# Dilated attention in pairs of heads: 64-row score products and eight units of work in place of sixteen

## What is computed

```python
n = rms_norm(h, ln_mix_g[l])
proj = n @ w_in[l]
qa, ka, va, qb, kb, vb, ga, gb = jnp.split(proj, splits, axis=-1)
qa = rope(qa.reshape(b, s, A_HEADS, HEAD_DIM), pos)      # 12 heads of 64
ka = rope(ka.reshape(b, s, A_HEADS, HEAD_DIM), pos)
ya = dilated_mixture(qa, ka, va).astype(h.dtype) @ w_branch_a[l]
```

## Time and profile before

| | |
|---|---|
| median of 3 runs | 3610.61 us |
| lowest, highest | 3605.58, 3610.79 us |
| span of the profiled execution | 3613.3 us |
| TensorE, VectorE, ScalarE busy | 3363.9, 1851.0, 1178.6 us |
| mean granted TensorE clock | 0.959 |

### The profile page before, as it was taken

The page is one execution under the profiler, slowest core; times in us unless marked ns, Lnnn a source line. Parts: engine busy times, 40 slices in busy tenths (PEclk is TensorE's granted clock), DMA queues, the critical chain, the costliest instruction groups (busy, mean ns, idle before and its releaser), DMA issues. The chain is left out here.

```text
span 3613.3 us, 51777 instructions
## 1 busy us (share of the span) xinstructions
PE 3363.9 (93%) x22874; PEld 2722.1 (75%) x22874; DVE 1851.0 (51%) x2262; ACT 1178.6 (33%) x1475; POOL 71.9 (2%) x50
## 2 busy tenths in 40 slices
PE   8999998999999999999999979999698778899996
PEld 7777777788778887987788857888376766588885
DVE  5344565677344435363644265443744765654436
ACT  3224544322232223432322243222323333232223
POOL 0000000000000001000100011000000000100001
PEclk9898999999999999999999999999698899899998
DMA  4111122222222223222222322322122000122231
GB/s 156 59 36 35 47 105 82 73 103 86 89 93 94 101 88 114 82 82 99 83 104 83 104 70 82 105 83 86 43 82 80 4 4 15 53 94 100 84 107 47
DMA packets 44463, 283.71 MB, mean 79 GB/s; under 512 B 5184, under 2 KB 5456, under 8 KB 18384
## 3 DMA queue, kind: packets, MB, share of 16 engines
q1 hardware_dynamic: 44240, 280.41, 22.5%
HBM read 278.29 MB, written 2.10 MB: 78 GB/s over the span
## 5 line engine op out<-in xcount | busy, mean ns | idle before, releaser
L460 PE MATMUL ps<-xh,wh 128*128 128x512 f32 x2464 | 982.4, 399 | 86.0 <-DVE xl L935 34.9
L460 PE MATMUL ps<-xl,wh 128*128 128x512 f32 x2464 | 971.3, 394 | 0.0
L460 PE MATMUL ps<-xh,wl 128*128 128x512 f32 x2464 | 970.7, 394 | 0.0
L313 DVE TENSOR_TENSOR wl<-raw,wh 128x2048 fp32r<-128x2048 f32 (+3 forms) x284 | 591.3, 2082 | 465.2 <-ACT wh L308 464.9
L460 PEld LDWEIGHTS ps<-xh,wh 128*128 128x128 f32 x2464 | 467.5, 190 | 217.1 <-issue 85.4
L308 ACT CAST wh<-raw 128x2048 fp32r<-128x2048 f32 (+3 forms) x284 | 492.1, 1733 | 307.3 <-PE ps L460 302.0
L460 PEld LDWEIGHTS ps<-xh,wl 128*128 128x128 f32 x2464 | 467.6, 190 | 102.1 <-issue 2.7
L460 PEld LDWEIGHTS ps<-xl,wh 128*128 128x128 f32 x2464 | 468.5, 190 | 97.5 <-issue 2.4
L460 PE MATMUL ps<-hid_h,wh 128*128 128x512 f32 x880 | 346.1, 393 | 2.7 <-DVE wl L313 2.7
L460 PE MATMUL ps<-hid_h,wl 128*128 128x512 f32 x880 | 346.4, 394 | 0.0
L460 PE MATMUL ps<-hid_l,wh 128*128 128x512 f32 x880 | 346.0, 393 | 0.0
(11 more groups left out here) (382 smaller groups left out, 4020.4 us busy)
## 6 DMA issues: line engine op xcount, KB each, us to landing
raw<-in_up SPq DMA_DIRECT2D x88, 1024.0 KB, 4.9
raw<-in_down SPq DMA_DIRECT2D x64, 704.0 KB, 4.0
raw<-in_up_c SPq DMA_DIRECT2D x22, 1024.0 KB, 4.8
raw<-in_down_c SPq DMA_DIRECT2D x16, 704.0 KB, 4.1
raw<-in_gates SPq DMA_DIRECT2D x8, 1024.0 KB, 4.9
raw<-in_gv SPq DMA_DIRECT2D x8, 1024.0 KB, 4.9
raw<-in_gu SPq DMA_DIRECT2D x8, 1024.0 KB, 4.9
raw<-in_gout SPq DMA_DIRECT2D x8, 1024.0 KB, 4.9
```

Of the source, the lines that this page charges most:

```text
L313: nc.vector.tensor_tensor(wl[:, slot, 0:w], raw[:, slot, 0:w], wh[:, slot, 0:w].bitcast(F32), ALU.subtract).then_inc(lo_ready, 1)
L460: last = nc.tensor.matmul(out, stationary, moving, start=(fresh and q == 0), stop=(t == kt - 1 and half == per - 1 and q == 2), skip_group ...
```

## The change

`rotate` writes its two results into a new buffer, `turned_rows`. ScalarE then issues eight DMAs per chunk of q or k, 48 in all, which copy 32 rows each into `qk` so that each head has its two halves below each other in 64 rows: heads 0 and 2 of a group in rows 0 to 63, heads 1 and 3 in rows 64 to 127 of two tiles. A score is then one product of 64 rows. The units become 8, of a pair of heads and a block b, in the order b = 0, 3, 1, 2, each with 12 fill steps. Every step of a unit handles both heads: scores and `weigh` alternate between them, in different banks and row halves (scores) or in different column halves (`weigh`). The masks of a group are added to both heads' scores in one instruction. The exponentials, the normalising and the turning stay one per head; normalising is now in place. The scores of a unit are issued in two parts and each waits for the group two before it; the lots of a turn hold 2 to 4 blocks. In units 0 and 4 the split of the next chunk comes ahead of the copies and behind the mask.

```diff
-    rope = area("rope", [P, 2, T], 44 * KB)
-    dil = area("dil", [P, GROUPS, T + 384], 48 * KB)
+    dil = area("dil", [P, GROUPS, T + 384], 44 * KB)
+    turned_rows = area("turned_rows", [P, 2 * GROUPS, 2, T], 54 * KB + 512)
+    rope = area("rope", [P, 2, T], 78 * KB + 512)
...
-            nc.vector.tensor_tensor(tile(qk, k * 2 + first_tile), tmp[:, 0, :], tmp[:, 1, :],
+            nc.vector.tensor_tensor(turned_rows[:, first_tile // 2 + k, 0, :], tmp[:, 0, :], tmp[:, 1, :],
                                     ALU.subtract).then_inc(dve_steps.sem, 1)
...
+    def place_heads(first_tile):
+        def part(act, k, products, u):
+            act.wait_ge(dve_steps.sem, dve_steps.after(k, 6))
+            for half in range(2):
+                for j in range(GH):
+                    row = HD * (j % 2) + HD // 2 * half
+                    act.dma_start(qk[row:row + HD // 2, first_tile + 2 * k + j // 2, :],
+                                  turned_rows[32 * j:32 * j + 32, first_tile // 2 + k, half, :]).then_inc(heads_placed, 16)
+        return part
+
+    linear("qa", KD, 256, x_split, act_part=place_heads(0), dve_part=rotate(0), steps=(0, 6), norms=first_norm)
...
-    units = [(j, b) for j in range(GH) for b in range(TB)]
+    units = [(pair, b) for pair in range(GH // 2) for b in (0, 3, 1, 2)]
+    LAST = len(units) - 1
...
+    LOT_SIZES = {0: ([3], [3]), 1: ([3, 3], [3, 3]), 2: ([3, 3, 2], [3, 3, 2]), 3: ([4, 3, 3], [3, 4, 3])}
...
+    def turn_bank(lot, size):
+        return ps[:, 6, 0:size * P] if lot % 2 == 0 else ps[:, 7, P:P + size * P]
+
+    def score_bank(u, g, e):
+        return 1 + 2 * ((GROUPS * u + g) % 2) + e
...
+        pe.wait_ge(heads_placed, HEADS_PLACED)
...
+    def opens(u):
+        return u * PER % (2 * KD) == 0
+
     @block.tensor
     def _(pe):
+        def scores(u, g):
+            pair, b = units[u]
+            step = GROUPS * u + g
+            if step >= 2:
+                pe.wait_ge(da_masked.sem, da_masked.base + step - 1)
+            k0, n = key_span(g, b)
+            for e in range(2):
+                rows = slice(HD * e, HD * e + HD)
+                last = nc.tensor.matmul(ps[:, score_bank(u, g, e), 0:n], qk[rows, 2 * g + pair, b * P:(b + 1) * P],
+                                        qk[rows, 2 * GROUPS + 2 * g + pair, k0:k0 + n], start=True, stop=True)
             last.then_inc(da_scores.sem, 1)
+        def turn(u, e):
+            pe.wait_ge(da_norm.sem, da_norm.after(u, e + 1))
+            for lot, first_block, size in turn_lots(u, e):
+                if lot >= 2:
+                    pe.wait_ge(da_moved.sem, da_moved.base + lot - 1)
...
         def weigh(u):
...
+            for n, (g, kb_) in enumerate(every):
+                for e in range(2):
+                    head = (g * GH + 2 * pair + e) * HD
+                    last = nc.tensor.matmul(ps[HD * e:HD * e + HD, 7, 0:P], va[:, kb_, head:head + HD],
+                                            probs_t[:, e, n * P:(n + 1) * P], start=(n == 0), stop=(n == len(every) - 1),
+                                            skip_group_check=True)
...
+        scores(0, 0)
+        scores(0, 1)
+        fill(0, 0, 2)
+        scores(0, 2)
         for u in range(len(units)):
+            if u < LAST:
+                scores(u + 1, 0)
+                scores(u + 1, 1)
+            fill(u, 0 if u else 2, 5)
             turn(u, 0)
+            if u < LAST:
+                scores(u + 1, 2)
+            fill(u, 5, 8)
             turn(u, 1)
+            fill(u, 8, PER)
             weigh(u)
...
+                nc.vector.tensor_tensor(masked[u % 2][:, :, off[g]:off[g + 1]], score_pair(u, g, n),
+                                        dil[:, g, m0:m0 + n].unsqueeze(1).broadcast_to([P, 2, n]),
+                                        ALU.add).then_inc(da_masked.sem, 1)
...
         for u in range(len(units)):
             normalise(u)
+            if u < LAST:
                 mask(u + 1)
+            if opens(u):
+                rows_of, unit = begun(u)[0]
+                rows_of.low(dve, unit // 2)
             for rows_of, unit in ended(u):
                 if rows_of is not vb_tokens:
                     rows_of.evict(dve, unit)
             low(u)
```

More of the change, by code:

```diff
@@ L1355, in begun @@
         return LOTS[(u * PER + KD - 1) // KD:((u + 1) * PER + KD - 1) // KD]
+    def opens(u):
+        return u * PER % (2 * KD) == 0
     @block.tensor
     def _(pe):
[L1359 to L1369, removed]
-            last.then_inc(da_scores.sem, 1)
@@ new lines, in turn @@
+        def turn(u, e):
[3 more added lines that the diff above has]
+                    pe.wait_ge(da_moved.sem, da_moved.base + lot - 1)
+                if u and lot == lots_before[u] + 1:
+                    pe.wait_ge(da_low.sem, da_low.after(u - 1, 1))
+                bank = turn_bank(lot, size)
+                for n in range(size):
+                    c0 = (first_block + n) * P
+                    last = nc.tensor.transpose(bank[:, n * P:(n + 1) * P], masked[u % 2][:, e, c0:c0 + P], table("ident"))
+                last.then_inc(da_turned.sem, 1)
@@ L1383, in weigh @@
         def weigh(u):
-            j, b = units[u]
-            pe.wait_ge(da_moved.sem, da_moved.after(u, 3))
+            pair, b = units[u]
+            pe.wait_ge(da_moved.sem, da_moved.base + lots_before[u + 1])
             if u:
                 pe.wait_ge(da_low.sem, da_low.after(u - 1, 1))
-            rows = slice(HD * (j % 2), HD * (j % 2) + HD)
-            every = [x for lot in key_blocks(b) for x in lot]
+            every = key_blocks(b)
             for n, (g, kb_) in enumerate(every):
-                head = (g * GH + j) * HD
-                last = nc.tensor.matmul(ps[rows, 7, 0:P], va[:, kb_, head:head + HD],
-                                        probs_t[:, n * P:(n + 1) * P], start=(n == 0), stop=(n == len(every) - 1))
+                for e in range(2):
[3 more added lines that the diff above has]
+                                            skip_group_check=True)
@@ L1435, in normalise @@
             n = offsets(units[u][1])[3]
-            dve.wait_ge(da_exp.sem, da_exp.after(u, 1))
-            nc.vector.reciprocal(stat[:, u % 2, 3:4], stat[:, u % 2, 2:3]).then_inc(da_rec.sem, 1)
+            dve.wait_ge(da_exp.sem, da_exp.after(u, 2))
+            nc.vector.reciprocal(stat[:, u % 2, 3, :], stat[:, u % 2, 2, :]).then_inc(da_rec.sem, 1)
             dve.wait_ge(da_rec.sem, da_rec.after(u, 1))
[L1439 to L1442, removed]
+            for e in range(2):
+                nc.vector.tensor_scalar(masked[u % 2][:, e, 0:n], masked[u % 2][:, e, 0:n], stat[:, u % 2, 3, e:e + 1], None,
+                                        ALU.mult).then_inc(da_norm.sem, 1)
         def low(u):
-            j, b = units[u]
-            rows, cols = slice(HD * (j % 2), HD * (j % 2) + HD), slice(b * P, (b + 1) * P)
+            pair, b = units[u]
+            cols = slice(b * P, (b + 1) * P)
             dve.wait_ge(da_high.sem, da_high.after(u, 1))
-            nc.vector.tensor_tensor(ya_l[rows, j // 2, cols], ps[rows, 7, 0:P], ya_h[rows, j // 2, cols].bitcast(F32),
+            nc.vector.tensor_tensor(ya_l[:, pair, cols], ps[:, 7, 0:P], ya_h[:, pair, cols].bitcast(F32),
                                     ALU.subtract).then_inc(da_low.sem, 1)
@@ L1459, in _ @@
             low(u)
-            for rows_of, unit in begun(u):
+            for rows_of, unit in begun(u)[1 if opens(u) else 0:]:
                 if unit % 2 == 0:
@@ L1468, in exps @@
             act.wait_ge(da_max.sem, da_max.after(u, 2))
-            nc.scalar.activation(masked[:, u % 2, 0:n], masked[:, u % 2, 0:n], ACT.Exp, bias=stat[:, u % 2, 1:2],
-                                 scale=SCALE, accum_out=stat[:, u % 2, 2:3]).then_inc(da_exp.sem, 1)
+            for e in range(2):
+                nc.scalar.activation(masked[u % 2][:, e, 0:n], masked[u % 2][:, e, 0:n], ACT.Exp,
+                                     bias=stat[:, u % 2, 1, e:e + 1], scale=SCALE,
+                                     accum_out=stat[:, u % 2, 2, e:e + 1]).then_inc(da_exp.sem, 1)
         exps(0)
         for u in range(len(units)):
[L1474 to L1483, removed]
+            pair, b = units[u]
+            if opens(u):
+                rows_of, unit = begun(u)[0]
+                rows_of.high(act, unit // 2)
+            for e in range(2):
+                for lot, first_block, size in turn_lots(u, e):
+                    act.wait_ge(da_turned.sem, da_turned.base + lot + 1)
+                    if lot == lots_before[u] and u:
+                        act.wait_ge(da_out.sem, da_out.after(u - 1, 1))
+                    nc.scalar.copy(probs_t[:, e, first_block * P:(first_block + size) * P],
+                                   turn_bank(lot, size)).then_inc(da_moved.sem, 1)
+            if u < LAST:
                 exps(u + 1)
@@ L1486, in _ @@
                 if rows_of is vb_tokens:
+                    if unit == 0:
```

(11 more changed lines are left out.)

70 lines of the change are left out of this document (31 added, 39 removed).

## The result

The changed kernel takes 3562.97 us (median of 4 runs, 3559.13 to 3565.76), the kernel before, measured beside it, 3610.7 (median of 4 runs, 3605.58 to 3615.28): a ratio of 0.9868, with a 95% interval of 0.9856 to 0.9879, or 47.7 us less. The forecast was 3558, 52.5 us less.

The account below looks back on a forecast made before the run. TensorE, busy 93% of the span, was taken as the bound. Dilated attention falling from 184.6 to 126.1 us (-58.5) plus 6 for placing the heads gave -52.5: 3610.6 to 3558 us, range 3540 to 3590, forecast chance 0.58.

Parts of the forecast that it names:

- placing the heads: Ahead of dilated attention: eight ScalarE DMA issues per chunk, 3.9 us, delay the weight split at five places; +6 us, 13 at slowest.
- scores at the full clock: Dilated attention: halved score columns, 64-row products of two heads overlapping by factor 0.545; 47.1 to 12.9 us, saving 34.2.
- `weigh`: Value products in dilated attention: 216 records, two heads alternating column halves; 23.8 to 13.0 us, saving 10.8.
- switches, seen at the fill: TensorE changing between part and all of its array, about 0.2 us each: 3 x 16 before, 5 x 8 after; 1.6 us less.
- waits within the stage: TensorE idle in dilated attention: 10 us against 5.7, from splits between units 5.8, turns' third lots 3.2, start 1.
- clock in the stage: Dilated attention: 12 us at the lower level (1.2 GHz) in place of 44.4, a loss of 6 us against 22.2.
- stages ahead: Stages before dilated attention: ScalarE's DMA issues make five weight chunks, first of ka to second of va, late; +6 us.
- Rival (b): Dilated attention: the two heads do not overlap, 64-row products filling all 128 output columns; stage 150.6 us, total 3583; chance 0.14.
- Rival (c): Dilated attention: the ScalarE and VectorE chain becomes the bound, 4 us at each of 7 hand-overs; +28, total 3586; chance 0.08.
- Rival (a): Dilated attention: the clock falls as often as before, 0.88; stage 136.5 us, total 3569; chance 0.14.
- the ring: Unforecast loop ahead of attention: rotation, eight issues, split_hi, split_lo, next rotation; 13.27 us a chunk against 10.88 of products.
- Rival (d): q, k, v stages: a ScalarE issue holds its queue until its transfer lands; at 2.7 us, total +36, 3647; chance 0.03.

## Why the prediction was right, step by step

The mechanism was as forecast in the stage. The total is 5 us off by the medians and 1.8 by the spans, and that it is so near is luck: placing the heads cost 8.2 us more than forecast, while the clock and `weigh` gave 6.4 more. Against the spans, in us:

| term | forecast | measured |
|---|---|---|
| scores at the full clock | -34.2 | -34.2 |
| `weigh` | -10.8 | -12.9 |
| switches, seen at the fill | -1.6 | -1.7 |
| waits within the stage | +4.3 | +4.9 |
| clock in the stage | -16.2 | -20.5 |
| stages ahead | +6 | +14.2 |
| behind the stage | 0 | -1.0 |

The first three are times from the start of one TensorE record to the start of the next, without idle time, at the lower clock halved: 49.1 to 14.9, 26.0 to 13.1, 72.5 to 70.8. The waits are idle time, 6.4 to 7.0, and 4.3 more hidden among the transposes, which go from 9.6 to 13.9 us. The remainder of half a microsecond is rounding between the views.

**Scores.** Right in its size and in its reason. The factor taken from L3145 was 0.545, the measured one is 0.53; the run on the same rows shows that the overlap is worth 8.5 us of it in the stage. Rival (b) falls. The Trainium skill, TensorEngine Tiling (Array Packing), section Tiling Modes, has such halves load and multiply independently, and this trace agrees: records of the score line start in pairs 7 ns apart.

**`weigh`.** Right in kind, 2 us short: the term took 23.8 us for before, from the rate within a series, and left out the start of each of sixteen series, of which eight are left.

**Waits.** The third lots came to 3.3 us for 3.2 forecast. The first lots that wait for VectorE's normalising came to 3.3 us, four waits, for the 5.8 given to splits between units. Rival (c), at 28 us, falls with them.

**Clock.** The direction was right and the amount 4 us short. Of the reasons given, one holds (32 of 128 rows) and two do not by themselves (the length of the series, the fill behind it). The 12 us at the lower level were an estimate without a row behind them. Rival (a) falls with the profile's 0.99.

**Placing the heads** is the term that was mis-sized: +6 us forecast, measured +14.2, outside its own bound of 13. The step that failed first is the price of an issue: eight were taken at 3.9 us, 0.49 each, from a series on SP whose members ran from 0.33 to 0.65; eight of one kind in a row cost 5.0, near the upper end of 5.2. The 1.1 us more, at five places, make 5.5 of the 8.2 missing. The waits came at five places, as forecast, but at 2.1 to 3.3 us each where 1 to 2 were forecast. Their sum is the chain's own at the measured price: 6 + 5.5 is 11.5, the ring gives 5 x 2.39 = 12, the view of waits 12.3. What the forecast did not say is why nothing is caught up in between, which is the ring. Of the 14.2, another 1.8 us TensorE shows as busy (108.23 against 106.43); the modelled end of the record before each wait and the slower record behind it are the likely reason. The Trainium skill, DMA: Bandwidth & Descriptors, section Issuing engines are not separate DMA queues, calls the issue time usually small beside the transfer; here eight issues last 5.0 us and one such transfer lands after 2.0, and the run that moved them off the ring took 12 us off the kernel. The measurement decides. Rival (d) falls: the next issue follows after 0.63 us, long before the 2.0 us of a landing.

## What to carry to other kernels

Cost a row of DMA issues like any other instruction of the engine whose queue holds them, and ask what stands behind them; the same 48 issues cost 14 us ahead of a split and half a microsecond behind it. Where a late step delays its own next input, work out the period of the ring, not the slack of one pass. And when products of 32 rows fill a stage, read the granted clock beside them: raising them to 64 rows may bring back clock on top of the columns that it saves (here 20.5 us beside 34.2).

## What the runs showed of the hardware that was not expected

- A 64 KB issue between two places in SBUF takes 0.63 us in a row of eight on ScalarE and 0.62 on SP; a load issued right behind such a row takes 0.58, where the quickest issue of the earlier trace rows takes 0.33.
- Streaming the same columns in the same order, twice as many rows cost no time by themselves and kept the clock up: score products over 32 rows went with 54.6 us at the lower level, over 64 rows with 3.4.
- TensorE seems to start a product of the other row half beside the running one although it stands four records further down its queue: pairs 7 to 14 ns apart, 16.3 us of series for 16.4. With the column halves of `weigh` the heads one behind the other did not overlap: 4.20 us for 2.40.
